# Head norms of the first layer's queries and keys, moved into the attention loop

## What is computed

```
q = rms_norm(q.reshape(n, t, A_HEADS, HEAD_DIM), p['q_norm_a'][a])      # 12 heads of 64
k = rms_norm(k.reshape(n, t, A_KV_HEADS, HEAD_DIM), p['k_norm_a'][a])   # 4 heads
o = swa_prompt(q, k, v, slopes, sinks)        # window of 128, blocks of 128 queries
xq = rms_norm(xq.reshape(n, t, X_HEADS, HEAD_DIM), p['xq_norm'][i])     # 4 heads
xo = memory_attention(xq, mk, mv)             # 256 memory tokens
x = x + jnp.concatenate([o, xo], axis=-1) @ w_out
```

## Time and profile before

| | |
|---|---|
| median of 3 runs | 2333.0 us (2332.85 to 2338.72) |
| the profiled execution | 2337.83 us |
| its span, first to last instruction | 2336.1 us |
| mean granted TensorE clock | 0.989 of full |
| TensorE busy | 2271.8 us, 97% |
| VectorE busy | 1123.9 us, 48% |
| ScalarE busy | 663.0 us, 28% |
| head norms, first spread to last multiplication | 222.3 to 238.1 us |
| attention of layer 0, first scores to the next projection | 239.2 to 367.8 us |

### The profile page before, as it was taken

The page is one execution under the profiler, slowest core; times in us unless marked ns, Lnnn a source line. Parts: engine busy times, 40 slices in busy tenths (PEclk is TensorE's granted clock), DMA queues, the critical chain, the costliest instruction groups (busy, mean ns, idle before and its releaser), DMA issues.

```text
span 2336.1 us, 38221 instructions
## 1 busy us (share of the span) xinstructions
PE 2271.8 (97%) x14742; PEld 2174.6 (93%) x14742; DVE 1123.9 (48%) x2138; ACT 663.0 (28%) x1205; POOL 599.6 (26%) x432
## 2 busy tenths in 40 slices
PE   5999899999999999999999999999999999999999
PEld 4898568989999999999999986998999999999998
DVE  7313574355455545445553134345545554454554
ACT  6211685431112221112243214443111222111211
POOL 3121453422122222112252212342112222211221
PEclk9999899999999999999999998999999999999999
DMA  6213101121111111111111112012101111111112
GB/s 207 84 54 112 40 2 30 37 64 37 36 45 54 54 54 36 36 45 45 54 46 54 37 37 99 31 36 63 44 29 52 47 54 54 39 41 36 45 54 87
DMA packets 36292, 123.35 MB, mean 53 GB/s; under 512 B 5264, under 2 KB 9968, under 8 KB 34896
## 3 DMA queue, kind: packets, MB, share of 16 engines
q1 hardware_dynamic: 29680, 106.25, 14.4%
q10 hardware_dynamic: 6528, 15.94, 1.8%
HBM read 115.57 MB, written 8.63 MB: 53 GB/s over the span
## 4 chain that ended last, share of the span: by engine, by line
PE 88%; DVE 5%; issue 4%; ACT 1%; POOL 1%; ACTq 0%; DVEq 0%; POOLq 0%
PE ps L522 27%; PE ps L523 27%; PE ps L524 27%; DVE h_lo L1373 2%; PE ps L752 2%; PE ps L783 1%; PE ps L764 1%; DVE z L1743 1%; PE ps L831 1%; PE ps L649 1%; PE ps L636 1%; POOL w_lo L394 0%; PE ps L814 0%; PE ps L834 0%; ACT s_exp L1134 0%
## 5 line engine op out<-in xcount | busy, mean ns | idle before, releaser
L522 PE MATMUL ps<-h_hi,w_hi 128*128 128x352 f32 x3120 | 1012.5, 325 | 15.9 <-DVE h_lo L1373 5.5
L523 PE MATMUL ps<-h_lo,w_hi 128*128 128x352 f32 x3120 | 1001.1, 321 | 0.0
L524 PE MATMUL ps<-h_hi,w_lo 128*128 128x352 f32 x3120 | 1000.5, 321 | 0.0
L394 POOL TENSOR_TENSOR w_lo<-raw,w_hi 128x1024 fp32r<-128x1024 f32 x138 | 345.8, 2506 | 1500.4 <-ACT w_hi L956 1500.4
L522 PEld LDWEIGHTS ps<-h_hi,w_hi 128*128 128x128 f32 x3120 | 586.1, 188 | 37.2 <-issue 21.4
L523 PEld LDWEIGHTS ps<-h_lo,w_hi 128*128 128x128 f32 x3120 | 587.2, 188 | 0.0
L524 PEld LDWEIGHTS ps<-h_hi,w_lo 128*128 128x128 f32 x3120 | 585.7, 188 | 0.0
L1663 DVE TENSOR_TENSOR x<-x,ps 128x352 f32<-128x352 f32 x528 | 270.8, 520 | 173.4 <-PE ps L524 172.6
L522 PE MATMUL ps<-g_hi,d_hi 128*128 128x352 f32 x1056 | 340.4, 322 | 3.5 <-DVE g_lo L1656 3.5
L523 PE MATMUL ps<-g_lo,d_hi 128*128 128x352 f32 x1056 | 339.9, 322 | 0.0
L524 PE MATMUL ps<-g_hi,d_lo 128*128 128x352 f32 x1056 | 339.8, 322 | 0.0
(11 more groups left out here) (177 smaller groups left out, 1734.0 us busy)
## 6 DMA issues: line engine op xcount, KB each, us to landing
raw<-in_w SPq DMA_DIRECT2D x182, 512.0 KB, 3.5
x<-in_x_t ACTq DMA_DIRECT2D x4, 1056.0 KB, 10.3
out_y<-x ACTq DMA_DIRECT2D x8, 528.0 KB
s_mk<-in_s_mk SPq DMA_DIRECT2D x2, 2048.0 KB, 9.2
s_mv<-in_s_mv SPq DMA_DIRECT2D x2, 2048.0 KB, 13.4
mem_x<-in_mem_t ACTq DMA_DIRECT2D x1, 1024.0 KB, 6.7
s_k<-in_s_k SPq DMA_DIRECT2D x2, 512.0 KB, 4.1
s_v<-in_s_v SPq DMA_DIRECT2D x1, 1024.0 KB, 15.7
```

What stands on the lines that cost most here:

```text
L394: pool.tensor_tensor(lo, raw[:, slot], hi.bitcast(F32), ALU.subtract).then_inc(prepped, 1)
L522: pe.matmul(out, a, hi_x(k), start=(first and n == 0), stop=False)
L523: pe.matmul(out, a, lo_x(k), start=False, stop=False)
L524: ins = pe.matmul(out, b, hi_x(k), start=False, stop=(last and n == len(ks) - 1))
```

## The change

The six pieces of the memory query tiles (8, 9) are spread and multiplied first, as before in five banks. The other 24 go into attention passes 0 to 7, three a pass, in the order keys (6, 7), then window queries (0 to 5), all through bank 7. A spread stands after the first scores, one after the turns and one after the second scores; VectorE's multiplications stand after the first maxima, after the reciprocal, and after the second maxima. Each spread in bank 7 waits for the multiplication before it. Scores of pair 0 wait for the six early pieces and four value groups. What needed all 30 pieces moves: POOL's bias to pass 7, the turn and copy of the new keys to pass 8, the filling of `s_k` and `q_pad` to VectorE's pass 9, and the ten sample steps to passes 10 to 19. SP's program is the same text; its waits for `z_normed` 30 and `turned_taken` 6 are met when these are.

The diff, with loops' unchanged lines left out:

```diff
+SPREAD_TILES = [8, 9, 6, 7, 0, 1, 2, 3, 4, 5]
+N_EARLY = 6
 def spreads_a():
-    return [(q // NCH, q % NCH, 1 + q % 5, q - 4 if q >= 5 else None) for q in range(30)]
+    early = [(SPREAD_TILES[q // NCH], q % NCH, 1 + q % 5, q - 4 if q >= 5 else None) for q in range(N_EARLY)]
+    return early + [(SPREAD_TILES[q // NCH], q % NCH, 7, q if q > N_EARLY else N_EARLY) for q in range(N_EARLY, 30)]
-SAMPLE_AT = (4, 0)
+SAMPLE_AT = (10, 0)
...
@@ POOL @@
-                if l == 0:
-                    pool.wait_ge(m["z_normed"], 30)
-                    make_bias(0)
-                    make_bias(1)
                 pool.memset(sp_pad[:, :, :], 0.0).then_inc(m["ppad_zeroed"], 1)
                 for it, (kind, q, b) in enumerate(item_pairs(l)):
+                    if l == 0 and it == 7:
+                        pool.wait_ge(m["z_normed"], 30)
+                        make_bias(0)
+                        make_bias(1)
                     normalise(2 * it)
@@ TensorE @@
                 if step == "window scores":
+                    pe.wait_ge(m["turned_taken"], 6)
...
+            def spread_a(q):
+                m = mx[0]
+                s_i, c, bank, need = spreads_a()[q]
+                pe.wait_ge(m["z_rstd"], 1)
+                if q == N_EARLY:
+                    pe.wait_ge(m["turned_taken"], 5)
+                if need is not None:
+                    pe.wait_ge(m["z_normed"], need)
+                pe.matmul(ps[:, bank, 0:CH], sel_t[32 * c:32 * c + 32, s_i, :], rstd[32 * c:32 * c + 32, :],
+                          start=True, stop=True).then_inc(m["z_spread"], 1)
+            def turn_new_keys():
+                m = mx[0]
+                pe.wait_ge(m["z_normed"], 30)
+                for t in range(2):
+                    mm = pe.transpose(ps[0:TS, 7, t * P:(t + 1) * P], z[:, 6 + t, 0:TS], ident[:, :])
+                mm.then_inc(m["turned"], 1)
...
+                if l == 0:
+                    pe.wait_ge(m["z_normed"], N_EARLY)
+                    pe.wait_ge(m["turned_taken"], 4)
                 for it in range(M + 2):
+                    late = N_EARLY + 3 * it if l == 0 and it < 8 else None
+                    if l == 0 and it == 8:
+                        turn_new_keys()
                     if it < M:
                         scores(2 * it)
+                    if late is not None:
+                        spread_a(late)
                     if it >= 2:
                         turn(2 * (it - 2))
                         turn(2 * (it - 2) + 1)
+                    if late is not None:
+                        spread_a(late + 1)
                     if it < M:
                         scores(2 * it + 1)
+                    if late is not None:
+                        spread_a(late + 2)
                     if it >= 2:
                         values(2 * (it - 2))
...
-                    for s_i, c, bank, need in spreads_a():
-                        ...
+                    for q in range(N_EARLY):
+                        spread_a(q)
...
-                if l == 0:
-                    pe.wait_ge(m["z_normed"], 30)
-                    pe.wait_ge(m["turned_taken"], 5)
-                    for t in range(2):
-                        mm = pe.transpose(ps[0:TS, 7, t * P:(t + 1) * P], z[:, 6 + t, 0:TS], ident[:, :])
-                    mm.then_inc(m["turned"], 1)
-                    pe.wait_ge(m["turned_taken"], 6)
@@ ScalarE @@
                 for it in range(M + 2):
+                    if l == 0 and it == 8:
+                        act.wait_ge(m["turned"], 6)
+                        scopy(k_tok[:, :], ps[0:TS, 7, 0:256]).then_inc(m["turned_taken"], 1)
...
-                    act.wait_ge(m["turned"], 6)
-                    scopy(k_tok[:, :], ps[0:TS, 7, 0:256]).then_inc(m["turned_taken"], 1)
@@ VectorE @@
+            def normalise_a(q):
+                t, c, bank, _ = spreads_a()[q]
+                g_c = qgain[:, 0:1] if t < 6 else hgain[:, 1:2] if t < 8 else qgain[:, 1:2]
+                dve.wait_ge(mx[0]["z_spread"], q + 1)
+                zz = z[:, t, c * CH:(c + 1) * CH]
+                STT(out=zz, in0=zz, scalar=g_c, in1=ps[:, bank, 0:CH], op0=ALU.mult, op1=ALU.mult) \
+                    .then_inc(mx[0]["z_normed"], 1)
...
-                if l == 0:
+                def window_queries():
+                    dve.wait_ge(m["z_normed"], 30)
                     for i in range(2):
...
+                    if l == 0 and it == 9:
+                        window_queries()
+                    late = N_EARLY + 3 * it if l == 0 and it < 8 else None
                     if it < M:
                         top(2 * it)
+                    if late is not None:
+                        normalise_a(late)
                     if 1 <= it <= M:
                         scale(2 * it - 1)
+                    if late is not None:
+                        normalise_a(late + 1)
                     if it < M:
                         top(2 * it + 1)
+                    if late is not None:
+                        normalise_a(late + 2)
```

More of the change, by code:

```diff
@@ L874, in _ @@
                 if l == 0:
-                    pe.wait_ge(m["z_rstd"], 1)
-                    for s_i, c, bank, need in spreads_a():
[L878 to L881, removed]
+                    for q in range(N_EARLY):
+                        spread_a(q)
                 else:
@@ L1500, in prompt_attention @@
                     ins.then_inc(m["qpad_filled"], 1)
-                else:
+                if l == 1:
                     dve.wait_ge(m["qpad_zeroed"], 1)
@@ L1736, in _ @@
                     dve.reciprocal(rstd[:, :], root[:, :]).then_inc(m["z_rstd"], 1)
[L1738 to L1745, removed]
+                    for q in range(N_EARLY):
+                        normalise_a(q)
+                else:
+                    dve.wait_ge(m["z_normed"], 24)
                 if l == 1:
```

## The result

| | before | after |
|---|---|---|
| median, us | 2334.88 (2332.85 to 2338.72, 4 runs) | 2372.35 (2356.00 to 2373.74, 4 runs) |
| profiled execution, us (its span) | 2337.8 (2336.1) | 2373.74 (2372.0) |
| mean granted clock | 0.989 | 0.978 |

The ratio is 1.0143, 95% interval 1.0128 to 1.0157; the medians are 37.5 us apart (1.6%), and the one run of 2356.00 makes the ratio smaller. The changed kernel is slower, 2.4 us above the forecast of 2370 and inside its range.

A forecast was written before the change was run, and what follows sets the result against it. TensorE's own stream was taken as the bound almost everywhere, VectorE from 222.3 to 251.8 us. Terms +24.5 + 6.5 + 1.4 + 2.6 + 2.0 = +37.0 us gave 2370 us against the median 2333.0; range 2339 to 2376.

The forecast's parts named there:

- Front (1): Before attention: scores wait for six pieces, not 30, so they start near 226.3 instead of 239.19, 12.9 us earlier.
- Price and chain of spreads (2, 3): Pairs 0 to 7: 0.78 us per spread on TensorE; bank 7 waits hidden within 0.1, except in pairs 0 and 1.
- Clock (4): Memory pairs: granted clock falls near 228 and stays at 0.50 until the window pairs; chance 0.50.
- second rival: Memory pairs: clock never falls or is back before pair 2; 2336 us, or 2328 with cheaper spreads; chance 0.13.
- first rival: Memory pairs: clock falls but comes back in pair 2 or 3; 2345 to 2349 us; chance 0.33.
- Half-clock pair (5): Memory pairs at 0.50: 10.3 us each; pair 8 starts at 301.1 instead of 276.6, shift +24.5 us.
- Moved work (6): Behind pair 8: scores and turns moved there add +6.5 us, their two stalls of 1.01 and 0.41 add +1.4.
- Copies in pass 9 (7): Pair 9 on VectorE: sample's key and query copies make pair 10's values late, +2.6 us, bounds 0 and 4.3.
- Tail (8): Start of pair 8: lower clock lasts another 3 to 5 us at half speed, +2.0 us.
- Clock back in pair 2: Memory pairs: clock falls, returns in pair 2 or 3, then holds; 2345 to 2349 us; chance 0.33.
- Clock kept: Memory pairs: full clock throughout or before pair 2, TensorE only pays its spreads; +2.6, 2336 us; chance 0.13.
- Spreads nearly free: Memory pairs at full clock: spreads cost 0.39 us each, under their neighbours; 2321 to 2329 us; chance 0.04.

The follow-up runs named there:

- e3_extra: Kernel before plus 24 unused matmuls of a spread's shape, three in each of passes 16 to 23; 2352.72 us, ratio 1.0071.
- e2_warm: Changed kernel plus 13 unused full-height matmuls, behind the third and sixth spreads and in passes 0 and 1; 2342.52 us, ratio 1.0034.
- e1_rows96: Changed kernel with each spread multiplying 96 rows instead of 32, rstd laid out in three zero-padded blocks; 2345.91 us, ratio 1.0046.
- e9_free_pass: Changed kernel with its 24 late spreads six a pass in passes 0, 1, 3 and 5, none in 2, 4, 6, 7; 2370.81 us, ratio 1.0149.
- e4_sample: Kernel before with only the sample steps moved to pass 10 on and the s_k and q_pad copies to pass 9; 2336.44 us, ratio 1.0004.
- e7_before_warm: Kernel before plus eight unused full-height matmuls, one to three spreads from the seventh spread on; 2336.96 us, ratio 1.0006.
- e8_front: Changed kernel with all 30 pieces ahead of pair 2, first four blocks' scores among them, copies in passes 2 and 3; 2332.71 us, ratio 0.9988.

## Why the prediction held, step by step

- **Front (1).** First scores at 225.82; forecast 226.3. The gain of 12.9 us reads as 13.4 on the two traces' own axes; 0.5 of that lies ahead of the first spread, so it was 12.9.
- **Price and chain of spreads (2, 3).** 0.79 at the full clock (e3_extra), 0.78 as taken. The chain through bank 7 costs slightly more than the 0.1 I allowed: in e2_warm the pair is 5.84 against 5.64. In pairs 0 and 1 the chain is there, but only once a pair: the 1.7 us of the first line below are 0.76 at 228.13, 0.76 at 235.64 and 0.17 among the early spreads. Pairs 0 and 1 took 13.88 against the 13.1 walked. After's waits of TensorE (engine, line, who, total, times, longest):

```profile
PE ps L745 <- DVE z L1514: 1.7, 3, 0.8
PE ps L682 <- POOL s_p L478: 1.7, 1, 1.7
...
PE ps L776 <- DVE stat L1557: 0.8, 1, 0.8
```

- **Clock (4).** It fell at 227.1 (forecast near 228), never rose in the memory pairs, and came back in pair 8. This was the step that decided, and the row that carried it, 228 to 238 in the earlier trace rows, was read rightly: e1_rows96 shows that the spreads' rows matter, and e9_free_pass that it comes back where turns, scores and values have no spread among them. It was put at 0.50, so it was a judgement, not a certainty. The supporting row of layer 1 is weaker than it was made: between 1411.07 and 1413.88 its products are of 32 rows, not "full products". (The rule that the prediction gives to its second rival, the clock back early in pair 2, is the case of the first rival in its list.) The Trainium skill, "TensorE: Matmul & The Clock Gate", section "What's actually happening", sets the gate by how busy the engine has been. The 61.90 us of 61.90 at 0.50 do not agree, if busy means that the engine has a matmul in hand; in e1_rows96, as busy, it rose at 248.7 with nothing but more rows in each spread.
- **Half-clock pair (5).** 10.51 against 10.28; three spreads of 1.47 instead of 1.40 are the difference. Pair 2 at 239.70 (239.4), the turn of the new keys at 302.77 (301.1); counted from the first spread these are 0.8 and 2.2 later than forecast.
- **Moved work (6).** Its sum stands (e4_sample: nothing net). One of its two stalls was mis-sized: 1.67 instead of the 0.41 of the earlier trace rows. POOL's timeline after shows what stands ahead of the sample's norm:

```profile
330.74 0.89 POOL L461 TENSOR_SCALAR bias<-nd_p 128x256 f32<-128x256 f32 x2
331.73 1.15 POOL L478 TENSOR_SCALAR s_p<-s_p,s_stat 128x160 f32<-128x160 f32 x3
```

  At its new place the step follows a bias tile (0.89) that it did not follow before, and I had moved the stall without walking POOL's queue again. In e4_sample, which has the same place, the wait is 1.66, behind a bias tile too.
- **Copies in pass 9 (7).** I took +2.6; the stall is 0.82. VectorE's timeline after:

```profile
308.34 2.36 DVE L1457 COPY q_pad<-z 64x32 f32<-64x32 f32 x12
```

  The twelve copies took 2.36 us instead of the 3.60 of the earlier trace rows; 1.24 of the 1.8 are that; that the rest was hidden is argued. The stall is the same 0.82 in e4_sample.
- **Tail (8).** 302.77 to 305.64 at 0.50, some 1.4 us lost against the 2.0 forecast.
- **Sum.** Counted from the first spread, attention ends 37.95 later, forecast +37.0: +2.2 at the turn of the new keys and +1.3 of POOL, less 1.8 of the copies and 0.6 of the tail, give 38.1. So the mechanism was right, but that the total is within 1 us is partly luck: misses of +3.5 and -2.4 cancel. The span grew by 35.9 only. Of the difference, 0.5 is the earlier first spread, and some 1.5 arose in layer 1, where the clock was at 0.50 for 13.7 us before, from 1408.9, and for 10.2 in after; 3.4 us less at 0.50 is 1.7 us of time (an estimate). e7_before_warm and e4_sample, whose layer 1 is before's, have 10.2 there and 3.4 more later (from 1449.7 and from 1596.0), so I count it as scatter.
- **The rivals.** "Clock back in pair 2" is what e1_rows96 does: 2345.9, inside its 2345 to 2349. "Clock kept" was priced at 2336 and e2_warm took 2342.5. It is 7.5 over its own before, where the sum had +2.6, so 4.9 us were missing. Pair 2 starts 16.17 us after the first spread instead of 12.6 (+3.6; 3.3 of that is passes 0 and 1, which hold the added matmuls), six pairs have 0.2 more (+1.2), POOL's stall is +1.3, and the copies give back 1.8: that makes 4.3, and 0.6 stays open. So at the full clock the change would most likely still not have been a gain; no run has that clock without added matmuls. "Spreads nearly free" is excluded by e3_extra.

## What to carry to other kernels

Work that an engine does for nothing in the shadow of another one costs its full length once it is moved to a place where that engine is the bound: 18 spreads x 0.79 = 14.2 us here, against 12.9 us gained in front. Before moving short matmuls that use few rows, look at what the granted clock did in a stretch of them alone, and at what stretch brought it back; thinning them out over a long dense loop that starts at the lower level kept 78 us at half speed, while the same pieces in one lump cost 24 us of it. Interleave the other way round: a few pieces of the dense work into the stretch that another engine bounds, not the short pieces into the dense loop. e8_front does that and is 2.7 us under before, though the copies it also moves have a part in this.

## What was not expected of the hardware

- The same twelve 64x32 copies on VectorE took 3.60 us in front, where POOL was working on bias and padding, and 2.36 us in pass 9. One of the twelve took 1.21 us, beginning at 240.18, where POOL's memset of `sp_pad` ran from 240.19 to 241.36; in pass 9 the longest took 0.27. That fits POOL as the cause, but no run takes it away alone.
